# A third pair of r's tiles by seven products, and the mixer's pieces moved together into 44 chunks

## The chip, the cores and the metric

The kernel runs on one core of a Trainium2 chip. The metric is device time in microseconds (us) of one launch, the median of several runs. TensorE (PE) multiplies matrices, VectorE (DVE) and ScalarE (ACT) work elementwise, GpSimd (POOL) does little here, and SyncE (SP) issues nearly all transfers. Each engine takes its instructions strictly in the order in which they were written; semaphores order the engines among each other.

## The reference, cut to what matters

One decoder layer over T = 544 tokens (512 new, 32 sampled), width 2048, fp32. What the change touches is the mixer: a wide input projection whose columns feed gated linear attention (q, k, v, r and a low-rank decay), a short convolution and a chunk MLP.

```python
proj = xn @ w_in
q, k, v, r, a_lr, cb, cc, ch, cu, cv = jnp.split(proj, _split_idx(), axis=-1)
loga = jax.nn.log_sigmoid((a_lr @ w_a2 + b_a).astype(jnp.float32)) / GLA_TAU
o, S_new = gla_chunked((q * (GLA_DK ** -0.5)).reshape(...), k.reshape(...), v.reshape(...), loga.reshape(...), S0)
o = o * lax.rsqrt(jnp.mean(o * o, axis=-1, keepdims=True) + EPS)
o = o * gla_g.reshape(GLA_HEADS, GLA_DV).astype(jnp.float32)
o_gla = o.reshape(B, L, D_GLA).astype(xn.dtype) * jax.nn.silu(r)
...
u = jax.nn.gelu(cu, approximate=False)
vv = layernorm(jax.nn.gelu(cv, approximate=False), cm_ln_g, cm_ln_b)
zc = jnp.einsum('hts,bnshc->bnthc', Wm, vb) + jnp.transpose(cm_bs[:, :T])[None, None, :, :, None]
o_cm = u * zc.reshape(B, L, D_CM)
out = jnp.concatenate([o_gla, o_conv, o_cm], axis=-1) @ w_out
```

Behind it come the residual, a SwiGLU with 5632 hidden columns, and a last norm.

## The kernel before

**Precision.** Every fp32 weight block is split into a rounded high part (ScalarE, a cast into `w_hi`) and a remainder (VectorE, a subtraction into `w_lo`). Each product is then three matmuls: high by high, high by low, low by high.

**The input projection comes in two forms.** A *tile* is 128 output columns. An ordinary tile takes two *chunks* of 8 weight blocks (`tile_half`, `chunk`). One chunk is 8 x 3 x 2 = 48 matmuls over 272 tokens each, so two tiles are four chunks, 192 matmuls. A *seven-product slot* (`kv_product`) does a pair of tiles at once: 12 of the 16 row blocks by Strassen's seven products (7 x 6 x 3 = 126 matmuls), the other four directly in an eighth step (4 x 4 x 3 = 48), together 174. `NR` slots hold tiles of r, six hold k and v; `NQ = NR + 6`. The tiles of r that go through slots are sent to DRAM (`r_dram`) and fetched back later into the last `2 * NR` tiles of `trunk`; ScalarE applies Silu to them there (`R_AT`), and VectorE multiplies them into the attention's output one chunk later, counting `front_done`. The other tiles of r are the last ordinary ones (from `T_R`), with Silu in `gate_tile`.

**The mixer's small work stands between the chunks.** From chunk `C_T` to `C_OUT` TensorE runs the ordinary tiles 17 to `N_IN - 1`. A table of places (`VT_AT`, `Z_AT`, `B_AT`, ...) puts *pieces* of the attention and the chunk MLP behind certain chunks; a place with .5 is the middle of the next chunk. TensorE does a piece's matmuls (`piece`), then VectorE and ScalarE their part (`post`), and `post_v` and `post_a` count what is done. The order that a piece waits for is set in `piece`: `mu` waits for all pieces ahead of it, `("s", 0)` for all up to `var_cm`, `("qs", 0)` for all up to `kdt` and for `s0_split`.

The pieces spoken of below:
- `z0`, `z1`: decay logits. `b0` to `b4`: cumulated decays, transposes and scores. `kdt`: the last transposes of k.
- `qs0` to `qs7`: old state by queries. The state is loaded to `S0` in eighths and split into `s0_hi` (`split_s0_hi`) and `s0_lo` (`split_s0_lo`); these stand at the end of the step two chunks ahead of each `qs`. The first `split_s0_hi` waits for `kdt`, since its room was in use until then.
- `mu`, `var_cm`: mean and variance of the chunk MLP's layer norm.
- `s0`, `s1`: scores and output of the sampled tokens; `s2` to `s9`: the new state. `vvt`, `zc`: chunk MLP. `p0` to `p3`: attention of the pairs. `on0` to `on3`: the heads' norm.

In its step for chunk c, VectorE waits for that chunk's last matmul, takes the finished tile out of PSUM if c is odd (`evac`; one tile in three of the convolution's is followed by `conv_tile`), does the pieces' parts, splits the weights of chunk c + 4 and then a part of the state. So what TensorE waits for can stand behind other work of that queue.

**Transfers.** SyncE issues all of them in program order, waits included, so a transfer that must wait holds up those behind it. Near `C_OUT` the input x is fetched back into `trunk` (`x_back`), in pieces of four tiles.

Of the kernel before, what the change touches and what calls it, by code (L numbers as in the profile page):

```python
# [28 lines left out]
ALU = mybir.AluOpType  # L29
# [4 lines left out]
KT = D // P  # L34
# [16 lines left out]
T_Q, T_CV, T_CONV, T_CU, T_R, N_IN = 1, 17, 21, 33, 37, 41  # L51
# [7 lines left out]
NR = 2  # L59
# [5 lines left out]
C_T = C_Q + NPQ * NQ  # L65
# [20 lines left out]
HEAD_ORDER = (2, 3, 0, 1)  # L86
# [7 lines left out]
B_AT = tuple(C_T + 5 + 2 * i for i in range(5))  # L94
KDT_AT = C_T + 15
QS_AT = tuple(C_T + 17 + i for i in range(8))
MU_AT, VAR_CM_AT, VVT_AT, ZC_AT = C_T + 19.5, C_T + 21.5, C_T + 26, (C_T + 27, C_T + 28)
S_AT = (C_T + 23, C_T + 25) + tuple(C_T + i for i in (29.5, 30.5, 31.5, 32.5, 33.5, 35, 36, 37.5))
P_AT = tuple(C_T + 29 + i for i in range(4))
OSQ_AT = C_T + 32  # L100
ON_AT = tuple(C_T + i for i in (34, 36.5, 38, 40))
# [52 lines left out]
def build(nc, xT, w_alr, w_in, w_kv, w_kc, w_oa, w_out, w_gu, w_d4, w_d3, vecs, wa2, wm, wsbd, bs, s0, cbuf, ident, tri, maskA, maskS,  # L154
          bmask, yT, gla_p, gla_s, conv_o, cmv):
    with ExitStack() as ctx:
# [289 lines left out]
        def slot_out(s):  # L446

            return kv[:, s + 4 if s < NR else s - NR]
# [74 lines left out]
        def _(sp):  # L523
# [96 lines left out]
            for c in range(C_T, C_OUT):  # L620
# [3 lines left out]
                if c == C_T + 13:  # L624
                    sp.wait_ge(inter, number(("z", 1)))
                    load_s0(0)
                    load_s0(1)
                if c == C_T + 14:
                    sp.wait_ge(inter, number(("z", 1)))
                    sp.dma_start(wmm, wm).then_inc(wm_in, 16)  # L630
                    sp.dma_start(bsb, bs.partition_broadcast(P)).then_inc(wm_in, 16)
                for i in range(8):
                    if c == QS_AT[i] + 5:
                        load_s0((i + 2) % 8, (i + 2) // 8)
                    if c == math.ceil(S_AT[2 + i] + 6.5):
                        store_s0(i)
                if c == P_AT[-1] + 10:
                    sp.wait_ge(post_v, parts(V_KINDS, ("p", PAIRS - 1)))
                    sp.dma_start(gla_p.rearrange("h d e -> d h e"), S[:]).then_inc(stored, 16)
                    for i in range(3):  # L640
                        sp.dma_start(trunk[:, 4 * i:4 * i + 4, :], xT[:, 4 * i:4 * i + 4, :]).then_inc(x_back, 16)
# [4 lines left out]
                if c == C_OUT - 1:  # L646
                    sp.wait_ge(front_done, 2 * NR)
                    sp.dma_start(trunk[:, 12:, :], xT[:, 12:, :]).then_inc(x_back, 16)
# [8 lines left out]
                for i in range(6):  # L657
                    if c == math.ceil(S_AT[2 + i] + 6.5):
                        load_s0(i + 2, 1)
# [163 lines left out]
        def _(act):  # L823
# [89 lines left out]
            def gate_tile(i, function):  # L913
                take()
                nc.scalar.activation(tmp[:, i % 2, :], tmp[:, i % 2, :], function).then_inc(silu_r, 1)
# [77 lines left out]
            def op_hi_tile(k):  # L993
                act.wait_ge(mix_done, k - 3)
                act.wait_ge(chunk_done, C_OUT)
                nc.scalar.copy(op_hi[:, k, :], mix[:, MIX_ORDER[k], :]).then_inc(op_h, 1)
# [860 lines left out]
        def _(dve):  # L1857
# [145 lines left out]
            def post(kind, i):  # L2003
# [132 lines left out]
                elif kind == "qs":  # L2136
                    if i % 2 and i < 7:
                        last = query_blocks(i // 2 + 1)
# [140 lines left out]
            def kv_outputs(s, piece):  # L2279
# [3 lines left out]
                if piece == C11:  # L2283
                    if s >= NR + 4:
                        dve.wait_ge(r_out, 16 * (s - NR - 3))
# [135 lines left out]
            for c in range(C_T, C_OUT):  # L2421
# [26 lines left out]
                if c == R_AT + 1:  # L2448
                    dve.wait_ge(post_v, parts(V_KINDS, ("on", 1)))
                    for i in range(2 * NR):  # L2450
                        dve.wait_ge(r_act, i + 1)
                        nc.vector.tensor_tensor(mix[:, 4 + i, :], mix[:, 4 + i, :], trunk[:, KT - 2 * NR + i, :],
                                                ALU.mult).then_inc(front_done, 1)
# [508 lines left out]
```

## Time and profile before

| | |
|---|---|
| median of 3 runs | 2175.64 us (2175.28 to 2175.84) |
| profiled execution, whole | 2175.7 us |
| its span | 2173.9 us |
| TensorE busy | 2163.2 us, 100% of the span |
| VectorE / ScalarE busy | 1707.1 us (79%) / 1014.1 us (47%) |
| seven-product slots | about 64.3 to 238.5 us |
| ordinary tiles with the mixer's pieces | about 238.5 to 590.9 us |
| output projection, first half by seven products | about 590.9 to 675.6 us |

The profiled execution is 1.8 us longer than its span, which is what lies around the first and last instruction. Read the table from the top: an engine at 100% sets the time, and the others matter only where they make it wait. Shares over the whole span hide this, so the stretch of the change has to be read by itself.

### The profile page before, as it was taken

The numbers are of one execution on the slowest core, as the hardware profiler recorded it, in microseconds if no ns is written. First come the engines' busy times: TensorE is split into PE (matmuls) and PEld (weight loads), VectorE is DVE, ScalarE is ACT, GpSimd is POOL, SyncE is SP. The second block draws the span as 40 slices with busy tenths as digits, with TensorE's granted clock in tenths as the row PEclk, the third lists the DMA queues.
The fourth block names the chain that finished last, engine by engine and source line by source line (L and its number), as shares of the span: only waits on it lengthen the run. The fifth ranks groups of instructions, "written<-read, shape, count | busy, mean of one in ns | idle before, by whom it ended". The sixth has DMA issues, their size and how long they took to land.

```text
span 2173.9 us, 40813 instructions
## 1 busy us (share of the span) xinstructions
PE 2163.2 (100%) x17270; PEld 2157.9 (99%) x17270; DVE 1707.1 (79%) x2005; ACT 1014.1 (47%) x1352; POOL 11.6 (1%) x16
## 2 busy tenths in 40 slices
PE   9999999999999999999999999999999999999998
PEld 9999999999999999999999999999999999999998
DVE  7766567656696799878888887888888888887887
ACT  8333352315454555444444544444444445444455
POOL 0000000000000000000000000000000000000001
PEclk9999999999999999999999999999999999999999
DMA  5332233327333434444445445444544885555523
GB/s 192 107 119 86 92 107 117 109 89 256 109 107 108 148 131 153 126 154 156 141 142 159 143 131 159 153 132 142 160 151 157 298 301 213 192 200 190 207 88 131
DMA packets 123167, 328.90 MB, mean 151 GB/s; under 512 B 10878, under 2 KB 51646, under 8 KB 121888
## 3 DMA queue, kind: packets, MB, share of 16 engines
q1 hardware_dynamic: 122224, 326.80, 44.7%
q8 instruction: 85, 1.39, 0.3%
q10 hardware_dynamic: 816, 0.37, 0.1%
q14 instruction: 42, 0.34, 0.0%
HBM read 269.39 MB, written 57.74 MB: 150 GB/s over the span
## 4 chain that ended last, share of the span: by engine, by line
PE 97%; DVE 1%; ACT 1%; issue 1%; DMA 0%; POOL 0%; POOLq 0%; DVEq 0%; ACTq 0%
PE acc L1736 24%; PE acc L1416 20%; PE g L1736 18%; PE acc L1744 12%; PE g L1744 9%; PE acc L1645 3%; PE g L1645 2%; PE acc L1683 2%; PE g L1683 2%; PE g L1637 1%; PE acc L1637 1%; PE g L1443 0%; PE g L1585 0%; PE g L1571 0%; PE g L1578 0%
## 5 line engine op out<-in xcount | busy, mean ns | idle before, releaser
L1221 ACT CAST w_hi<-w_s 128x1024 fp32r<-128x1024 f32 (+1 forms) x204 | 209.1, 1025 | 359.0 <-DVE w_s L2544 350.5
L1736 PE MATMUL g<-op_hi,w_hi 128*128 128x272 f32 x1056 | 272.1, 288 | 0.0
L1736 PE MATMUL acc<-sg_hi,w_hi 128*128 128x272 f32 x1056 | 272.0, 288 | 0.0
L1736 PE MATMUL g<-op_lo,w_hi 128*128 128x272 f32 x1056 | 271.9, 288 | 0.0
L1736 PE MATMUL acc<-op_hi,w_hi 128*128 128x272 f32 x1056 | 271.6, 288 | 0.0
L1736 PE MATMUL acc<-sg_lo,w_hi 128*128 128x272 f32 x1056 | 271.4, 288 | 0.0
L1736 PE MATMUL acc<-op_lo,w_hi 128*128 128x272 f32 x1056 | 271.4, 288 | 0.0
L2519 DVE TENSOR_TENSOR w_lo<-w_s,w_hi 128x1024 fp32r<-128x1024 f32 (+1 forms) x204 | 242.5, 1189 | 12.6 <-ACT w_hi L1221 6.4
L1416 PE MATMUL acc<-op_hi,w_hi 128*128 128x272 f32 x1152 | 241.5, 291 | 0.1
L1416 PE MATMUL acc<-op_hi,w_lo 128*128 128x272 f32 x1152 | 238.3, 288 | 0.0
L1416 PE MATMUL acc<-op_lo,w_hi 128*128 128x272 f32 x1152 | 238.2, 288 | 0.0
L1736 PEld LDWEIGHTS acc<-sg_lo,w_hi 128*128 128x128 f32 x1056 | 198.7, 188 | 0.1
L1736 PEld LDWEIGHTS acc<-op_hi,w_hi 128*128 128x128 f32 x1056 | 198.6, 188 | 0.1
L1736 PEld LDWEIGHTS g<-op_lo,w_hi 128*128 128x128 f32 x1056 | 198.7, 188 | 0.0
L1736 PEld LDWEIGHTS g<-op_hi,w_hi 128*128 128x128 f32 x1056 | 198.5, 188 | 0.1
L1736 PEld LDWEIGHTS acc<-op_lo,w_hi 128*128 128x128 f32 x1056 | 198.6, 188 | 0.0
L1736 PEld LDWEIGHTS acc<-sg_hi,w_hi 128*128 128x128 f32 x1056 | 198.5, 188 | 0.1
L2519 DVE TENSOR_TENSOR w_lo<-w,w_hi 128x1024 fp32r<-128x1024 f32 (+1 forms) x126 | 150.4, 1193 | 49.1 <-ACT w_hi L1221 48.1
L1416 PEld LDWEIGHTS acc<-op_hi,w_hi 128*128 128x128 f32 x1152 | 181.3, 188 | 1.4 <-issue 0.3
L1416 PEld LDWEIGHTS acc<-op_hi,w_lo 128*128 128x128 f32 x1152 | 180.6, 189 | 0.0
L1416 PEld LDWEIGHTS acc<-op_lo,w_hi 128*128 128x128 f32 x1152 | 180.2, 188 | 0.0
L1221 ACT CAST w_hi<-w_raw 128x1024 fp32r<-128x1024 f32 (+1 forms) x115 | 118.4, 1030 | 95.6 <-PE acc L1744 82.7
(395 smaller groups left out, 4882.0 us busy)
## 6 DMA issues: line engine op xcount, KB each, us to landing
w<-w_gu SPq DMA_DIRECT2D x88, 512.0 KB, 3.3
w_raw<-w_gu SPq DMA_DIRECT2D x88, 512.0 KB, 4.1
w_raw<-w_in SPq DMA_DIRECT2D x55, 512.0 KB, 3.5
hf_dram<-hf_hi SPq DMA_DIRECT2D x22, 952.0 KB, 6.4
hf_dram<-hf_lo SPq DMA_DIRECT2D x22, 952.0 KB, 8.7
w_raw<-w_d SPq DMA_DIRECT2D x34, 512.0 KB, 4.0
w<-w_d SPq DMA_DIRECT2D x26, 512.0 KB, 3.3
op_hi<-hf_dram SPq DMA_DIRECT2D x16, 544.0 KB, 7.0
```

The lines of the kernel that those rows point to most:

```text
L1221: nc.scalar.copy(w_hi[:, (C_ST + n) % RING, 0:w], src[:, 0:w]).then_inc(hi_ready, 1)
L1416: last = nc.tensor.matmul(acc[t % 2][:, a, 0:TH], w, x[:, k, a * TH:(a + 1) * TH], start=start and n == 0, stop=stop and n == 2)
L1637: last = nc.tensor.matmul(bank[:, side, 0:TH], w, x, start=False, stop=j == KT - 2 * HQ - 1 and i == 2, skip_group_check=True)
L1645: last = nc.tensor.matmul(banks[idx][:, side, 0:TH], w, x, start=idx < 2 and j == 0 and i == 0, stop=j == HQ - 1 and i == 2, skip_group_ch ...
L1683: last = nc.tensor.matmul(out, w, x, start=idx < 2 and j == 0 and i == 0, stop=j == HP - 1 and i == 2, skip_group_check=True)
L1736: nc.tensor.matmul(out, w_h, x, start=fresh and j == 0 and i == 0, stop=False, skip_group_check=True)
L1744: last = nc.tensor.matmul(out, w_l, x_h, start=False, stop=j == h - 1, skip_group_check=True)
L2519: nc.vector.tensor_tensor(w_lo[:, slot, 0:w], src[:, 0:w], f32(w_hi[:, slot, 0:w]), ALU.subtract)\
```

## The change

`NR` goes from 2 to 3: six of r's eight tiles now go through slots, two stay ordinary. So `N_IN` falls from 41 to 39, there are nine slots in place of eight, and `C_T` to `C_OUT` holds 44 chunks in place of 48. The pieces are moved together into the 44: from `b2` on they stand earlier, and some distances shrink. `kdt` to `qs0` was two chunks and is one. `mu` stood half a chunk behind `qs2` and stands half a chunk behind `qs3`. `var_cm` to `s0` was a chunk and a half and is half a chunk. The places of `z0`, `z1`, `b0` and `b1` (3, 6, 5 and 7) are as before. Tiles that return from DRAM are six, the multiplications by them six; the last head is now head 0 (`HEAD_ORDER`); x comes back as two pieces of four tiles early and two late, where it was three early and one late. Silu's table is loaded ahead of the wait in `gate_tile`.

```diff
-T_Q, T_CV, T_CONV, T_CU, T_R, N_IN = 1, 17, 21, 33, 37, 41
+T_Q, T_CV, T_CONV, T_CU, T_R, N_IN = 1, 17, 21, 33, 37, 39
-NR = 2
+NR = 3
-HEAD_ORDER = (2, 3, 0, 1)
+HEAD_ORDER = (2, 3, 1, 0)
 Z_AT = (C_T + 3, C_T + 6)
-B_AT = tuple(C_T + 5 + 2 * i for i in range(5))
-KDT_AT = C_T + 15
-QS_AT = tuple(C_T + 17 + i for i in range(8))
-MU_AT, VAR_CM_AT, VVT_AT, ZC_AT = C_T + 19.5, C_T + 21.5, C_T + 26, (C_T + 27, C_T + 28)
-S_AT = (C_T + 23, C_T + 25) + tuple(C_T + i for i in (29.5, 30.5, 31.5, 32.5, 33.5, 35, 36, 37.5))
-P_AT = tuple(C_T + 29 + i for i in range(4))
-OSQ_AT = C_T + 32
-ON_AT = tuple(C_T + i for i in (34, 36.5, 38, 40))
+B_AT = tuple(C_T + i for i in (5, 7, 8.5, 10, 11.5))
+KDT_AT = C_T + 13
+QS_AT = tuple(C_T + 14 + i for i in range(8))
+MU_AT, VAR_CM_AT, VVT_AT, ZC_AT = C_T + 17.5, C_T + 19.5, C_T + 23, (C_T + 24, C_T + 25)
+S_AT = (C_T + 20, C_T + 22) + tuple(C_T + i for i in (26.5, 27.5, 28.5, 29.5, 30.5, 32, 33, 34.5))
+P_AT = tuple(C_T + 26 + i for i in range(4))
+OSQ_AT = C_T + 29
+ON_AT = tuple(C_T + i for i in (31, 32.5, 34, 35.5))
 R_AT = C_T + 36
...
-                if c == C_T + 13:
+                if c == C_T + 14:
                     sp.wait_ge(inter, number(("z", 1)))
                     load_s0(0)
...
-                    if c == math.ceil(S_AT[2 + i] + 6.5):
+                    if c == min(math.ceil(S_AT[2 + i] + 6.5), C_OUT - 4):
                         store_s0(i)
...
-                    for i in range(3):
+                    for i in range(2):
                         sp.dma_start(trunk[:, 4 * i:4 * i + 4, :], xT[:, 4 * i:4 * i + 4, :]).then_inc(x_back, 16)
...
                     sp.wait_ge(front_done, 2 * NR)
-                    sp.dma_start(trunk[:, 12:, :], xT[:, 12:, :]).then_inc(x_back, 16)
+                    for i in (2, 3):
+                        sp.dma_start(trunk[:, 4 * i:4 * i + 4, :], xT[:, 4 * i:4 * i + 4, :]).then_inc(x_back, 16)
...
             def gate_tile(i, function):
+                if i == T_R - T_CU:
+                    load_tables(ACT.Silu)
                 take()
...
                 elif kind == "qs":
+                    if i in (4, 6):
+                        dve.wait_ge(post_v, parts(V_KINDS, (("mu", 0) if i == 4 else ("var_cm", 0))))
                     if i % 2 and i < 7:
                         last = query_blocks(i // 2 + 1)
...
                 if c == R_AT + 1:
-                    dve.wait_ge(post_v, parts(V_KINDS, ("on", 1)))
+                    dve.wait_ge(post_v, parts(V_KINDS, ("on", 2)))
```

The order in which instructions stand, at three places, all on VectorE. First, around `kdt` and the first part of the state, before. `L1875` splits weights, `L1944` and `L2183` take a tile out, `L1951` to `L2058` are `kdt`'s part, `L1985` to `L1981` prepare the queries, `L1988` is the low part of the state:

```order
L1875 TENSOR_TENSOR w_lo<-w_raw,w_hi 128x1024 [waits hi_ready,chunk_done]
L1944 TENSOR_TENSOR tmp<-acc,rstd 128x544 [waits mix_done,chunk_done]
L1951 CAST kd<-g 32x512 [waits inter]
L1952 CAST kd<-g 32x512
L1954 TENSOR_TENSOR kd<-g,kd 32x512 [waits v_own]
L1954 TENSOR_TENSOR kd<-g,kd 32x512
L2058 TENSOR_TENSOR egp<-egp 128x4x4 [waits v_own]
L1875 TENSOR_TENSOR w_lo<-w_raw,w_hi 128x1024 [waits hi_ready]
L1985 MEMSET qm 128x1088
L1980 CAST qm<-trunk 128x8x4 [waits v_own]
L1981 TENSOR_TENSOR qm<-trunk,qm 128x8x4 [waits v_own]
L1988 TENSOR_TENSOR s_lo<-S,s_hi 128x1024 [waits s0_split_h]
```

and now (four to six lines further down in the file: `L1992` is the low part of the state, `L1955` to `L2062` `kdt`'s part, `L2243` the convolution's last product):

```order
L1879 TENSOR_TENSOR w_lo<-w_raw,w_hi 128x1024 [waits hi_ready,chunk_done]
L1989 MEMSET qm 128x1088
L1984 CAST qm<-trunk 128x8x4 [waits v_own]
L1985 TENSOR_TENSOR qm<-trunk,qm 128x8x4 [waits v_own]
L1992 TENSOR_TENSOR s_lo<-S,s_hi 128x1024 [waits s0_split_h]
L1948 TENSOR_TENSOR tmp<-acc,rstd 128x544 [waits chunk_done]
L2243 TENSOR_TENSOR mix<-mix,tmp 128x544 [waits acc_free]
L1955 CAST kd<-g 32x512 [waits inter]
L1956 CAST kd<-g 32x512
L1958 TENSOR_TENSOR kd<-g,kd 32x512 [waits v_own]
L1958 TENSOR_TENSOR kd<-g,kd 32x512
L2062 TENSOR_TENSOR egp<-egp 128x4x4 [waits v_own]
```

The low part of the state, and the tile behind it, moved from behind `kdt`'s part to ahead of it.

Second, ahead of `mu` (its first row is the one that waits for `inter` at the end), on VectorE before:

```order
L1944 TENSOR_TENSOR tmp<-acc,rstd 128x544 [waits chunk_done]
L2237 TENSOR_TENSOR mix<-mix,tmp 128x544 [waits acc_free]
L1875 TENSOR_TENSOR w_lo<-w_raw,w_hi 128x1024 [waits inter,hi_ready]
L1988 TENSOR_TENSOR s_lo<-S,s_hi 128x1024 [waits s0_split_h]
L2061 SCALAR_TENSOR_TENSOR mix<-g,mix 128x544 [waits inter]
```

and now, from the convolution's taps on (`L2201` to `L2207`), with `qs3`'s part as `L1984` and `L1985`:

```order
L2201 TENSOR_SCALAR mix<-zp,vec 128x512 [waits v_own]
L2204 SCALAR_TENSOR_TENSOR mix<-zp,vec,mix 128x512 [waits v_own] x2
L2201 TENSOR_SCALAR mix<-zp,vec 128x32 [waits v_own]
L2204 SCALAR_TENSOR_TENSOR mix<-zp,vec,mix 128x32 [waits v_own] x2
L2206 COPY cst<-zp 128x2 [waits v_own]
L2207 COPY cst<-zp 128x16
L1984 CAST qm<-trunk 128x8x4 [waits inter]
L1985 TENSOR_TENSOR qm<-trunk,qm 128x8x4 [waits v_own]
L1879 TENSOR_TENSOR w_lo<-w_raw,w_hi 128x1024 [waits hi_ready]
L1992 TENSOR_TENSOR s_lo<-S,s_hi 128x1024 [waits s0_split_h]
L2065 SCALAR_TENSOR_TENSOR mix<-g,mix 128x544 [waits inter]
```

A whole convolution tile and a part of a `qs` piece now stand right ahead of `mu`.

Third, behind `var_cm`, on VectorE before (`L2079` and `L2084` are its part):

```order
L2079 SCALAR_TENSOR_TENSOR mix<-mix,vec,lnb 128x544 [waits post_a,inter]
L2079 SCALAR_TENSOR_TENSOR mix<-mix,vec,lnb 128x544 x3
L2084 TENSOR_SCALAR mix<-mix,vec 128x544 [waits v_own]
L2084 TENSOR_SCALAR mix<-mix,vec 128x544 x3
L1980 CAST qm<-trunk 128x8x4 [waits inter,chunk_done]
L1981 TENSOR_TENSOR qm<-trunk,qm 128x8x4 [waits v_own]
L1875 TENSOR_TENSOR w_lo<-w_raw,w_hi 128x1024 [waits hi_ready]
L1988 TENSOR_TENSOR s_lo<-S,s_hi 128x1024 [waits s0_split_h]
L1944 TENSOR_TENSOR tmp<-acc,rstd 128x544 [waits chunk_done]
```

and now, where `s0`'s part (`L2150` to `L2153`) follows at once:

```order
L2083 SCALAR_TENSOR_TENSOR mix<-mix,vec,lnb 128x544 [waits post_a,inter]
L2083 SCALAR_TENSOR_TENSOR mix<-mix,vec,lnb 128x544 x3
L2088 TENSOR_SCALAR mix<-mix,vec 128x544 [waits v_own]
L2088 TENSOR_SCALAR mix<-mix,vec 128x544 x3
L2150 COPY ovm<-idn 32x128 [waits post_v,chunk_done,inter]
L2150 COPY ovm<-idn 32x128
L2152 MEMSET ovm 32x128
L2153 COPY_PREDICATED ovm<-mS,g 32x128 [waits v_own]
```

Five instructions and a chunk that stood between `var_cm` and `s0` are gone from there.

## Rows read from the trace of the kernel before

**Rows 1.** The page's busy time of each engine.

```profile
PE 2163.2 (100%) x17270; PEld 2157.9 (99%) x17270; DVE 1707.1 (79%) x2005; ACT 1014.1 (47%) x1352; POOL 11.6 (1%) x16
```

**Rows 2.** Waits of TensorE: engine, line, releaser: us in total, times, longest.

```profile
PE g L1436 <- POOL onesf L797: 1.2, 1, 1.2
PE g L1829 <- DVEq L2850: 0.3, 1, 0.3
```

**Rows 3.** Chain of waits in time: start, us, what. Slots, then a chunk.

```profile
81.61 4.48 PE g L1645 x36
...
103.39 4.48 PE g L1645 x36
...
238.55 6.02 PE acc L1416 x48
```

**Rows 4.** Chain of waits: kdt, qs0, half a chunk, var_cm, three products.

```profile
351.94 0.44 PE g L1475 x4
...
364.41 0.97 PE g L1585 x8
...
394.24 3.03 PE acc L1416 x24
397.26 0.92 PE g L1468 x4
...
597.27 9.04 PE acc L1683 x72
```

**Rows 5.** VectorE in order of time: start, us, line, operation [idle before].

```profile
337.20 0.72 DVE L1944 TENSOR_TENSOR tmp<-acc,rstd 128x544 f32<-128x544 f32 x1 [0.41 <-PE acc L1416]
337.96 0.72 DVE L2237 TENSOR_TENSOR mix<-mix,tmp 128x544 f32<-128x544 f32 x1
...
352.62 0.67 DVE L1951 CAST kd<-g 32x512 fp32r<-32x512 f32 x1
...
355.43 0.17 DVE L2058 TENSOR_TENSOR egp<-egp 128x16 f32<-128x16 f32 x1
...
360.81 1.22 DVE L1988 TENSOR_TENSOR s_lo<-S,s_hi 128x1024 fp32r<-128x1024 f32 x1
```

**Rows 6.** ScalarE in order of time: high part of the state.

```profile
353.01 1.04 ACT L911 CAST s_hi<-S 128x1024 fp32r<-128x1024 f32 x1
```

**Rows 7.** VectorE in order of time: queries; then a convolution tile.

```profile
388.71 0.17 DVE L1980 CAST qm<-trunk 128x32 fp32r<-128x32 f32 x1
388.92 0.19 DVE L1981 TENSOR_TENSOR qm<-trunk,qm 128x32 fp32r<-128x32 f32 x1
...
408.21 0.72 DVE L1944 TENSOR_TENSOR tmp<-acc,rstd 128x544 f32<-128x544 f32 x1 [1.33 <-PE acc L1416]
...
413.12 0.44 DVE L2144 COPY ovm<-idn 32x128 f32<-32x128 f32 x2
```

**Rows 8.** VectorE in order of time: var_cm's part.

```profile
399.65 2.88 DVE L2079 SCALAR_TENSOR_TENSOR mix<-mix,vec,lnb 128x544 f32<-128x544 f32 x4 [2.81 <-ACT lnb L962]
402.56 1.74 DVE L2084 TENSOR_SCALAR mix<-mix,vec 128x544 f32<-128x544 f32 x4
```

**Rows 9.** VectorE in order of time: forms of the output projection.

```profile
565.03 1.29 DVE L2330 TENSOR_TENSOR fa_lo<-mix,fa_hi 128x1088 fp32r<-128x1088 f32 x1 [1.61 <-ACT fa_hi L1007]
...
598.77 1.29 DVE L2344 TENSOR_TENSOR op_lo<-mix,op_hi 128x1088 fp32r<-128x1088 f32 x1
```

**Rows 10.** Transfers from 480 to 600 us: KB each, median us to landing.

```profile
w_raw<-w_in SPq DMA_DIRECT2D x11, 512.0 KB, 3.8
trunk<-xT SPq DMA_DIRECT2D x4, 1088.0 KB, 9.8
```

**Rows 11.** Windows: length, busy PE, PEld, DVE, ACT, POOL, PEclk, DMA share, GB/s.

```profile
554.90:560.90 6.00, 6.00 (x50) 6.00 (x50) 2.68 (x3) 2.88 (x3) 0.00 (x0) 1.00 0.89 347
...
2165.00:2169.00 4.00, 0.00 (x0) 0.00 (x0) 3.22 (x6) 1.07 (x3) 2.82 (x3) 1.00 0.70 263
...
2170.00:2172.00 2.00, 0.00 (x0) 0.00 (x0) 0.00 (x0) 0.00 (x0) 0.10 (x1) 0.50 1.04 404
```

More of the change, by code:

```diff
@@ L446, in slot_out @@
         def slot_out(s):
-            return kv[:, s + 4 if s < NR else s - NR]
+            return kv[:, s + 6 - NR if s < NR else s - NR]
         def slot_kv(n):
@@ L627, in _ @@
                     load_s0(1)
-                if c == C_T + 14:
+                if c == C_T + 15:
                     sp.wait_ge(inter, number(("z", 1)))
@@ L657, in _ @@
                 for i in range(6):
-                    if c == math.ceil(S_AT[2 + i] + 6.5):
+                    if c == min(math.ceil(S_AT[2 + i] + 6.5), C_OUT - 4):
                         load_s0(i + 2, 1)
@@ L993, in op_hi_tile @@
             def op_hi_tile(k):
-                act.wait_ge(mix_done, k - 3)
+                if k < KT - 2:
+                    act.wait_ge(mix_done, k - 3)
                 act.wait_ge(chunk_done, C_OUT)
@@ L2283, in kv_outputs @@
                 if piece == C11:
-                    if s >= NR + 4:
-                        dve.wait_ge(r_out, 16 * (s - NR - 3))
+                    if s >= 6:
+                        dve.wait_ge(r_out, 16 * (s - 5))
                     nc.vector.tensor_tensor(y[:, 0, 0:TH], pa[:, q, 0:TH], rstd[:, 0:TH], ALU.mult).then_inc(kv_read, 1)
@@ L2448, in _ @@
                 if c == R_AT + 1:
-                    dve.wait_ge(post_v, parts(V_KINDS, ("on", 1)))
+                    dve.wait_ge(post_v, parts(V_KINDS, ("on", 2)))
                     for i in range(2 * NR):
                         dve.wait_ge(r_act, i + 1)
-                        nc.vector.tensor_tensor(mix[:, 4 + i, :], mix[:, 4 + i, :], trunk[:, KT - 2 * NR + i, :],
-                                                ALU.mult).then_inc(front_done, 1)
+                        m = mix[:, KT // 2 - 2 * NR + i, :]
+                        nc.vector.tensor_tensor(m, m, trunk[:, KT - 2 * NR + i, :], ALU.mult).then_inc(front_done, 1)
                 if c == MIX_SINGLE_AT:
```

## The prediction

> **What bounds the kernel now.** I read the busy times first. TensorE is busy 2163.2 of 2173.9 us [rows 1]. Then the waits of TensorE: there are two in the whole span, 1.2 us at the very start and 0.3 us near the end [rows 2]. So in all the stretches that the change touches TensorE never waits, and the time is the sum of its matmuls. What shortens its work shortens the kernel; what the other engines do counts only where a wait that was covered comes into the open. The chain of waits says the same: slot follows slot and chunk follows chunk with no gap [rows 3]. The profiled execution took 2175.7 us, 1.8 more than its span and 0.06 more than the median of 2175.64; I work from the former and take the 0.06 off at the end.
>
> **What is removed.** Slots repeat from 81.61 to 103.39 in the chain, 21.78 us each; the eight of them have one form. An ordinary chunk of 48 matmuls takes 6.02 us [rows 3]. Four chunks go, 24.08 us, and a slot comes, 21.78 us. That is -2.30 us on the engine that sets the end. By count it is 192 - 174 = 18 matmuls of 6.02 / 48 = 0.125 us, -2.26 us. I take -2.3. This is the most that the change can give, and it is 0.11% of the time, below the 0.2% (4.35 us) that a measurement of this kernel can tell from no change.
>
> The new slot costs VectorE and ScalarE more than four chunks' splits did, but they have idle time in that stretch and the slots before it had no gap, so I put it at nothing; from the eight slots as they ran it could be at worst a few tenths. The third pair to DRAM and the six Silus and products in place of four lie beside TensorE.
>
> **What is moved: every TensorE wait again.** The pieces stand closer, so for each I compared the moment when TensorE gets there with the moment when the queue ahead of the part it waits for is done, with the durations of before. Most keep a cover: the waits of the p and s pieces stand exactly as far apart as they did, and `b2`, `b3`, `b4`, `vvt` and `zc` arrive later than what they wait for. Three do not.
>
> *First, `qs0`, a chunk behind `kdt`.* It waits for `kdt`'s part on VectorE. The first cast of the state's high part on ScalarE waits for `kdt`'s matmuls; before, VectorE had `kdt`'s part ahead of the state's low part, now the low part is ahead, and with it the tile of that step. Counting from the end of `kdt`'s matmuls: the cast 1.04 [rows 6], with about 0.1 to start; the low part 1.22; the tile and its product 0.72 + 0.72; `kdt`'s part from 352.62 to 355.60, 2.98 [rows 5]. The sum is 6.8 us. TensorE is there after one chunk, 6.02 [rows 3]. Wait: 0.7 to 0.8, I take 0.7, since neighbours in the rows overlap by some 0.1. VectorE itself gets to the low part at about the time when the cast is done, because a convolution tile and `b4`'s part stand ahead in the same queue; where it is later, the wait grows by as much. Bounds 0.3 to 1.7.
>
> *Second, `mu`, half a chunk behind `qs3`.* It waits for all parts ahead, so for `qs3`'s. VectorE does that behind the tile of the step for `C_T + 17`, which is one with a convolution. Such a tile runs from 408.21 to 413.12, 4.91 us, and the queries take 388.71 to 389.11, 0.40 [rows 7]: 5.35 us from the chunk's end. TensorE is there after `qs3` and half a chunk, 0.97 + 3.03 = 4.0 [rows 4]. Wait: 1.4 with the release. Before, `mu` stood behind `qs2`, in a step without a convolution, and the wait was covered. Bounds 1.1 to 1.7.
>
> *Third, `s0`, behind `var_cm`, half a chunk and `qs6`.* It waits for `var_cm`'s part. `var_cm`'s matmuls ended at 398.18 [rows 4] and its last VectorE instruction at 404.30 [rows 8]: 6.12 us of square root by logarithm, then eight operations, all in a row. TensorE now gets there after 3.03 + 0.97 = 4.0. Wait: 2.15, with the release 2.2. Before, a whole chunk more stood between. Bounds 1.8 to 2.6.
>
> Behind `s0` VectorE has its own small part and a split, and the split is for a chunk four further on, so nobody else is held up. A wait also gives the other two engines time, so the three do not add to later ones.
>
> **Near `C_OUT`.** Six products with the returned tiles in place of four put VectorE some 1.3 us later at the handover, and with the tighter table I find the forms of the output projection (565.03, 26.0 us ahead of `C_OUT`) about 1.7 us later against it [rows 9]. The narrowest cover is the form for the fifth product. It was ready at 600.06 [rows 9]. TensorE started that product at 606.31 - 3.01 = 603.30, since the three products in the row end at 606.31 and take 9.04 [rows 4]: 3.2 us of cover. That leaves 1.5, so nothing. Loading Silu's table ahead gives time to a ScalarE that nobody waits for there: nothing. The same holds for the x tiles that now return late, with the proviso of the second rival.
>
> **Sum.** -2.3 + 0.7 + 1.4 + 2.2 = +2.0 us, 2177.7 on the profiled execution, 2177.6 as a median. The work that was saved is given back, and somewhat more, in three new waits. The title's word of second decay logits ahead of the second decay piece moves nothing: both places are as before.
>
> **A rule of the Trainium skill.** TensorE's clock was granted at 1.00, the 2.4 GHz level, in every stretch with matmuls that I looked at, and stayed at 1.00 over 4 us without a matmul, from 2165 to 2169 us at the kernel's end; it was 0.50, the 1.2 GHz level, from 2170 on [rows 11]. By that my longest wait, 2.2 us, leaves the clock where it is. The Trainium skill, in "TensorE: Matmul & The Clock Gate", section "Part 1: The HAM clock gate", says that the default is throttled and that activity releases it. It speaks against any change that opens gaps on TensorE; by the row, gaps of this length are not enough, and the trace does not show a gap between matmuls that would decide it.
>
> **Rivals.**
>
> *The waits are not there: 2173.4.* If VectorE's queue is ahead of my count, or the three waits stay under a few tenths each, the saving stands: 2175.64 - 2.3 = 2173.3 to 2175. For it: no wait of TensorE in this stretch in the trace [rows 2]. Against it: `mu` and `s0` are short by more than a microsecond, and their terms are a few instructions in a row with measured lengths.
>
> *The late x tiles hold up the last weights: slower, 2182.0.* SyncE now issues two transfers of 1088 KB behind `front_done`, about 27 us ahead of `C_OUT`, and the weights of the last chunk after them. If each took its 9.8 us after the other, and the weights 3.8 [rows 10], they would land 27.3 - 19.6 - 3.8 = 3.9 us ahead of `C_OUT`. They are needed 6.0 us ahead for the chunk, and 2.3 sooner for the splits (1.05 and 1.22), so 8.3. It would cost 4.4 us on top: 2182.0, which is slower by 0.29%. It decides from the point where the two take over 15 us together. Against it: 347 GB/s moved in the window in which the single one was under way [rows 11], and at that rate two take 6.4 us. The Trainium skill, in "DMA: Bandwidth & Descriptors", section "Issuing engines are not separate DMA queues", says that all transfers run on the same 16 DMA engines and interleave; by it the weights share with the x tiles even where they are not behind them. With the rate of the row both orders end in time.
>
> *The clock falls in a wait.* If a wait of 2 us brought the 1.2 GHz level, a chunk would take up to twice 6.02, so up to +6.0: 2183.6. The window behind the last matmul speaks against it.
>
> *The change doesn't do what it says.* The number of slots, chunks and pieces in the order of the instructions is as described, so I leave it no chance of its own.
>
> **How the numbers follow.** Forecast (three waits, 3.3 to 5.5 us together; 2176.3 to 2179.3): 0.60. No or small waits, 2173.3 to 2176.3: 0.22. Late x tiles, 2179.5 to 2182: 0.08. Clock: 0.02. Waits that I did not find, +1 to +5 on top: 0.08. The predicted time is 2177.6. The range runs from 2173.3, the whole saving, to 2181.0; it leaves out the upper part of the last three cases. Slower by over 0.2% (above 2180.0) takes most of the last three cases: 0.13. Faster by over 0.2% (below 2171.3) would need twice what the count of matmuls gives: 0.01. The rest, 0.86, is within 0.2%.
>
> **What would show it.** TensorE's matmuls fall by 18 in the whole, and nine slots of 21.8 us stand in the chain. Between `C_T` and `C_OUT`, TensorE's waits list three lines: the first matmul of `qs0` released by the last copy of `kdt`'s part, that of `mu` by the queries' subtraction, that of `s0` by `var_cm`'s last addition, with about 0.7, 1.4 and 2.2 us. The granted clock stays at 1.00 there. Wrong would be: no such lines; one of over 3 us; a wait for a transfer, or for weights, in the last chunks or at the first products of the output projection.

## The result and the profile after

The changed kernel takes 2180.08 us (median of 15 executions, 2178.06 to 2182.59), the kernel before 2175.64 (15 executions, 2175.24 to 2176.29). The ratio is 1.002, 95% interval 1.0013 to 1.0027: slower by 4.4 us, which is 0.2%. The forecast was 2177.6 with a range to 2181.0. The direction of the mechanism was right and its size too small. The profiled execution took 2180.65 us with a span of 2177.8; the three waits are in it as forecast, and three further terms are not in the forecast: longer pieces behind two of the waits, a low clock behind the third, and a longer output projection.

Busy times, against [rows 1]; 18 matmuls fewer, yet TensorE is busy as long as before:

```profile
PE 2163.1 (99%) x17252; PEld 2157.4 (99%) x17252; DVE 1714.7 (79%) x2016; ACT 1017.1 (47%) x1360; POOL 11.9 (1%) x16
```

TensorE's waits, against [rows 2]:

```profile
PE g L1596 <- DVE mix L2088: 2.2, 1, 2.2
PE g L1472 <- DVE qm L1985: 1.4, 1, 1.4
PE g L1440 <- POOL onesf L798: 1.2, 1, 1.2
PE g L1589 <- DVE egp L2062: 0.7, 1, 0.7
PE acc L1687 <- ACT acc L1032: 0.3, 1, 0.3
```

`s0` waits for `var_cm`'s last addition, `mu` for the queries, `qs0` for `kdt`'s last product: the three waits, their releasers and their lengths are those of the forecast. The fifth line is new: a seed that ScalarE copies for the output projection.

The chain at the second and third wait (start, us, what), against [rows 4]. It shows what the list of waits cannot: the pieces that follow a wait.

```profile
395.15 0.20 DVE qm L1985
...
395.40 1.18 PE g L1472 x4
396.58 3.02 PE acc L1420 x24
...
410.54 0.93 PE g L1472 x4
...
412.92 2.88 DVE mix L2083 x4
...
415.83 1.75 DVE mix L2088 x4
...
417.62 0.44 PE g L1596 x8
418.06 7.72 PE acc L1420 x48
425.79 0.96 PE g L1589 x8
```

The chunk behind `s0` takes 7.72 us where an ordinary one takes 6.02 [rows 3]. Behind `s0` the chunk is somewhat longer in the kernel before too, where no wait stands ahead of it:

```profile
409.13 0.37 PE g L1592 x8
409.50 6.24 PE acc L1416 x48
```

So about 1.5 us of the 7.72 are new. The windows over the chunk (length, busy PE, PEclk, DMA share, GB/s) say why:

```profile
417.00:418.00 1.00, 0.38 (x9) 1.00 0.00 0
418.00:419.00 1.00, 1.00 (x10) 1.00 0.00 0
419.00:420.00 1.00, 1.00 (x8) 0.61 0.07 16
420.00:421.00 1.00, 1.00 (x6) 0.50 0.00 0
421.00:422.00 1.00, 1.00 (x7) 0.50 0.59 115
422.00:423.00 1.00, 1.00 (x7) 0.69 0.97 385
```

The granted clock is still 1.00 when the wait ends, at 417.62, and for 1.6 us of matmuls behind it; then it is 0.50, the 1.2 GHz level. The four windows are short of 1.00 by 0.39, 0.50, 0.50 and 0.31 us of full clock, 1.7 together, which at half the clock is a stretch of 3.4 us (419.2 to 422.6). The chunk is longer by 1.5, nearly all of that.

**Where the time went, by stages.** Four instructions of TensorE mark the stages in every kernel: the first product of the first slot, the first product of the output projection that goes to `acc`, the first chunk product behind that projection's slots, and the first of the last group. In order of time (start, us, line, operation), before:

```profile
64.12 0.29 PE L1645 MATMUL acc<-op_hi,w_hi 128*128 128x272 f32 x1
...
591.10 0.29 PE L1683 MATMUL acc<-fa_hi,w_hi 128*128 128x272 f32 x1
...
675.41 0.42 PE L1416 MATMUL acc<-op_hi,w_hi 128*128 128x272 f32 x2
...
2163.35 1.54 PE L1829 MATMUL acc<-hst,onesf 128*128 128x272 f32 x6
```

and after:

```profile
64.08 0.29 PE L1649 MATMUL acc<-op_hi,w_hi 128*128 128x272 f32 x1
...
595.10 0.29 PE L1687 MATMUL acc<-fa_hi,w_hi 128*128 128x272 f32 x1
...
679.95 0.42 PE L1420 MATMUL acc<-op_hi,w_hi 128*128 128x272 f32 x2
...
2167.29 1.54 PE L1833 MATMUL acc<-hst,onesf 128*128 128x272 f32 x6
```

Stage A (slots, chunks and pieces) is the second start less the first: 526.98 before, 531.02 after, +4.04. Stage B (the output projection's slots) is 84.31 before, 84.85 after, +0.54. Stage C is 1487.94 and 1487.34; in the other kernels below it lies between 1487.33 and 1487.75. Half of the 0.6 is the wait of 0.3 us near the end [rows 2], which no other profile has; no experiment aims at the rest. Of the 5.0 us between the two profiled executions, 1.0 lies outside the span (2.9 us in place of 1.8). The table gives A and B of every profiled execution and the times of all; its last column is the kernel before, measured again beside that row.

| kernel | median us (lowest to highest) | A less 526.98 | B less 84.31 | before beside it |
|---|---|---|---|---|
| before | 2175.64 (2175.24 to 2176.29) | 0 | 0 | 2175.64 |
| after | 2180.08 (2178.06 to 2182.59) | +4.04 | +0.54 | 2175.64 |
| after, once more | 2180.53 (2178.39 to 2182.84) | +2.51 | +1.23 | 2175.45 |
| `s0` a chunk later | 2177.72 (2175.80 to 2178.23) | +0.24 | +0.66 | 2175.64 |
| `mu` waits for less | 2178.83 (2177.31 to 2179.51) | +2.37 | +1.22 | 2175.64 |
| `kdt`'s part first | 2180.04 (2178.17 to 2181.98) | +2.13 | +2.43 | 2175.64 |
| third wait alone | 2178.07 (2177.08 to 2180.73) | +0.49 | +1.73 | 2175.45 |
| all three mended | 2174.65 (2174.02 to 2176.62) | -1.80 | +0.54 | 2175.64 |
| the same, no table ahead | 2175.68 (2175.52 to 2177.22) | -1.80 | +2.00 | 2175.37 |
| the same, `r` sooner | 2177.05 (2175.75 to 2178.2) | -1.80 | +2.65 | 2175.45 |
| before, `s0` sooner | 2178.27 (2177.48 to 2180.58) | +2.21 | +0.01 | 2175.37 |
| `s0` ahead of `qs6` | 2182.2 (2179.21 to 2183.88) | +3.50 | +0.66 | 2175.37 |
| `s0` directly behind `var_cm` | 2185.62 (2185.03 to 2186.82) | +8.06 | +2.35 | 2175.37 |

The rows below "after" have eleven executions each, the last two six and five. One execution of 7470.4 us of the kernel with `s0` a chunk later, and one of 3006.76 us of the kernel before beside it, lie outside everything else and are left out of the ranges. One profile is one execution; its A and B show where that execution's time lies, and the median shows what is usual. Rows with different values in the last column are best compared by what each has over the kernel before beside it. The first slot starts between 64.08 and 64.57 in all of them, and what lies outside the span is 1.7 to 2.9 us.

### The profile page after: what moved, and what is told of

Read it like the earlier page. It is cut to its first block, busy times and chain, and to the rows that moved or that the text cites. A ratio compares the mean times of both kernels' runs of the same rounds, so it can differ in the third digit from the quotient of the medians.

```text
span 2177.8 us, 40793 instructions
## 1 busy us (share of the span) xinstructions
PE 2163.1 (99%) x17252; PEld 2157.4 (99%) x17252; DVE 1714.7 (79%) x2016; ACT 1017.1 (47%) x1360; POOL 11.9 (1%) x16
## 4 chain that ended last, share of the span: by engine, by line
PE 96%; DVE 2%; issue 1%; ACT 1%; DMA 0%; POOL 0%; POOLq 0%; DVEq 0%; ACTq 0%; SPq 0%
PE acc L1740 24%; PE g L1740 18%; PE acc L1420 17%; PE acc L1748 12%; PE g L1748 9%; PE acc L1649 4%; PE g L1649 3%; PE acc L1687 2%; PE g L1641 1%; PE acc L1641 1%; PE g L1687 1%; DVE w_lo L2312 0%; PE g L1447 0%; PE g L1575 0%; PE g L1582 0%
## 5 line engine op out<-in xcount | busy, mean ns | idle before, releaser
L1740 PE MATMUL acc<-op_hi,w_hi 128*128 128x272 f32 x1056 | 271.7, 289 | 0.0
L1740 PE MATMUL acc<-op_lo,w_hi 128*128 128x272 f32 x1056 | 271.5, 288 | 0.0
L1420 PE MATMUL acc<-op_hi,w_hi 128*128 128x272 f32 x1088 | 228.8, 292 | 0.0
L1420 PE MATMUL acc<-op_hi,w_lo 128*128 128x272 f32 x1088 | 225.9, 289 | 0.0
L1420 PE MATMUL acc<-op_lo,w_hi 128*128 128x272 f32 x1088 | 225.7, 289 | 0.0
L1740 PEld LDWEIGHTS acc<-op_lo,w_hi 128*128 128x128 f32 x1056 | 199.1, 189 | 0.0
L1740 PEld LDWEIGHTS acc<-op_hi,w_hi 128*128 128x128 f32 x1056 | 198.8, 188 | 0.1
L1420 PEld LDWEIGHTS acc<-op_hi,w_hi 128*128 128x128 f32 x1088 | 172.1, 189 | 1.1
L1420 PEld LDWEIGHTS acc<-op_hi,w_lo 128*128 128x128 f32 x1088 | 171.5, 190 | 0.0
L1420 PEld LDWEIGHTS acc<-op_lo,w_hi 128*128 128x128 f32 x1088 | 170.9, 189 | 0.0
```

The costliest lines, as they stand in the source:

```text
L1420: last = nc.tensor.matmul(acc[t % 2][:, a, 0:TH], w, x[:, k, a * TH:(a + 1) * TH], start=start and n == 0, stop=stop and n == 2)
L1740: nc.tensor.matmul(out, w_h, x, start=fresh and j == 0 and i == 0, stop=False, skip_group_check=True)
```

## Experiments

**The third wait.** `s0` one chunk later:

```diff
-S_AT = (C_T + 20, C_T + 22) + ...
+S_AT = (C_T + 21, C_T + 22) + ...
```

> Changed kernel with the matmuls of s0 one chunk later (at C_T + 21, behind qs7). My theory: the 2.2 us wait for var_cm's part goes, and with it the stretch at clock 0.50 that cost 1.7 us in the next chunk, so 3.9 us less than the changed kernel: 2176.2 as a median, the times within 0.5 us of each other, the granted clock 1.00 from 415 to 426 us, and the waits of qs0 (0.7) and mu (1.4) as they were. Rival A, the fall of the clock comes from the thin work of the whole stretch (three waits and short pieces), not from this wait: the clock still falls to 0.50 and only 2.2 us go, 2177.9. Rival B, the wait only moves to s1, now one chunk behind s0: no more than 1 us goes, 2179.

Measured: 2177.72, ratio to before 1.0009 (1.0000 to 1.0018). TensorE's waits between `C_T` and `C_OUT`:

```profile
PE g L1472 <- DVE qm L1985: 1.4, 1, 1.4
...
PE g L1589 <- DVE egp L2062: 0.7, 1, 0.7
```

The wait is gone and did not move to `s1`, so rival B falls. Every window from 414 to 428 us shows a clock of 1.00, which goes against rival A. Stage A is 3.80 less than after's, which is the 2.2 of the wait and the 1.5 of the low clock. As a median only 2.4 go, not the 3.9 that I expected. Not every execution of the changed kernel has the fall, as a later run shows. Nor are the times within 0.5 us of each other: four lie from 2175.80 to 2176.84, the profiled one among them, and six from 2177.62 to 2178.23, with a mean clock of 0.999. That speaks for something other than this wait and the clock, which makes some executions longer by about 1.5 us; the profile is of the shorter kind and can't name it.

**The second wait.** In the function that issues a piece:

```diff
+                elif kind == "mu":
+                    before = order[:number(("qs", 2))]
```

> Changed kernel with mu waiting for the parts up to qs2's in place of all parts ahead. My theory: the 1.4 us wait goes and nothing else changes: VectorE takes up mu's part at the same moment, so var_cm, s0 and the 2.2 us wait stand as they did or the wait grows a little, because TensorE comes sooner to it, by up to 1.4 us; the clock falls to 0.50 behind it as before. If var_cm's chain is bound by TensorE (its matmuls start it), 1.4 us go: 2178.7. Rival A, the waits stand in for one another (s0's end is set by VectorE): the wait at s0 grows by 1.4 and nothing goes, 2180.1. Rival B, the 1.4 us wait is part of what brings the clock down: the clock stays at 1.00 and 3.1 us go, 2177.0.

Measured: 2178.83, 1.2 us under the changed kernel. The wait is gone, and the third is as long as it was. The second line is `mu`'s piece in the chain:

```profile
PE g L1598 <- DVE mix L2090: 2.2, 1, 2.2
```

```profile
394.50 0.92 PE g L1472 x4
```

`mu`'s four products take 0.92 us here and 1.18 behind the wait. Stage A, with a fall in both profiles, is 1.67 less than after's: 1.4 for the wait and 0.26 for the piece.

Nor do the waits stand in for one another: `var_cm`'s part is started by TensorE's matmuls, so it starts sooner and ends sooner. Windows behind the wait (same columns):

```profile
416.00:417.00 1.00, 0.52 (x9) 0.87 0.00 0
417.00:418.00 1.00, 1.00 (x5) 0.50 0.08 16
...
420.00:421.00 1.00, 1.00 (x9) 0.92 0.70 160
```

The clock falls without `mu`'s wait ahead. So the 1.4 us wait is not needed for a fall, and rival B is out; the chunk takes 7.66 us. The wait ends at 416.48, and the window from 416 has 0.87: here the fall comes 0.3 us behind the wait's end, in the changed kernel's profile 1.6 us behind it.

**The first wait.** VectorE does `kdt`'s part before the low part of the first state; the zeroing of the queries stays where it was:

```diff
                     query_blocks(0)
+                    return
+                state_lo(i)
+
+            def state_lo(i):
                 dve.wait_ge(s0_split_h, i + 1)
...
+                if c == KDT_AT:
+                    state_lo(0)
                 split_lo(c + 4, c + 4)
```

> Changed kernel with VectorE doing kdt's part ahead of the low part of the first decode state, as in the kernel before. My theory: the queue from the end of kdt's matmuls to the end of what qs0 needs is tile 1.4, kdt's part 3.0, low part 1.2 = 5.6 us, under the chunk of 6.0: the 0.7 us wait goes and the others stay, 2179.4. Rival, the queue is longer by what stands in front of it on VectorE (a convolution tile and b4's part): a wait of 0.3 to 0.7 stays, 2179.8 to 2180.1.

Measured: 2180.04, no difference from the changed kernel's 2180.08, and where the rival put it. TensorE still waits 0.4 us at `qs0`, now for the low part. So the edit could bring some 0.3 us, and the profiled execution lost that elsewhere. In it the clock stayed at 1.00 behind the 2.2 us wait, and yet the time was 2180.96: stage B is 2.43 longer than before's. VectorE's waits from 500 to 582 us point at a decode state that landed late:

```profile
DVE S L2171 <- DMA S<-s: 2.3, 1, 2.3
```

and VectorE in order of time shows what became of it:

```profile
571.12 1.29 DVE L2340 TENSOR_TENSOR fa_lo<-mix,fa_hi 128x1088 fp32r<-128x1088 f32 x1 [1.99 <-ACT fa_hi L1011]
```

The forms start 22.46 us ahead of the first output product (593.58), where they start 24.24 ahead in the changed kernel and 26.07 in the one before. TensorE then waits 1.9 us for seeds. Two later profiles show the same: a state late by 1.7 us (third wait alone; forms 23.05 ahead, B +1.73) and by 2.2 us (`s0` directly behind `var_cm`; 22.58 ahead, B +2.35). In the two profiles of the changed kernel VectorE does not wait for a state at this place.

**All three.**

> All three edits at once: s0 one chunk later, mu waiting for qs2's part, kdt's part first on VectorE. My theory: no wait of TensorE is left between C_T and C_OUT, the clock stays at 1.00 there, and of the 4.3 us of waits and 1.7 us of clock nothing is left: 2175.64 - 2.3 for the slot in place of four chunks + 0.3 for the seed at the handover = 2173.6, faster than the kernel before by 0.09%. Rival A, the nine-slot form has a cost that no wait shows (more outside the span, a slower slot): 2175 to 2176. Rival B, the waits only move to the next pieces (s1, var_cm): 2176 to 2178.

Measured: 2174.65 (2174.02 to 2176.62), ratio 0.9998 (0.9989 to 1.0007); it is 1 us under before as a median, and that is not told from no change. TensorE's waits are all of these:

```profile
PE g L1440 <- POOL onesf L798: 1.2, 1, 1.2
PE acc L1420 <- ACT w_hi L865: 1.1, 1, 1.1
PE g L1591 <- DVE s_lo L1998: 0.4, 1, 0.4
PE acc L1689 <- ACT acc L1032: 0.3, 1, 0.3
```

The second is at the start of the kernel. Stage A is 1.80 less than before's, that is -2.3 for the slot in place of four chunks, 0.4 for the wait at `qs0` that is left and 0.2 for `qs0`'s first piece, which takes 1.18 us behind that wait and 0.97 before [rows 4]: -1.7, to 0.1 us. So the saving on TensorE is real and of the forecast size, and the waits were what ate it. Rival B falls: no wait moved. My time of 2173.6 was too low by 1.0 and rival A's, 2175 to 2176, too high by 0.35, and its reason doesn't hold: no slot is slower. Stage B is 0.54 longer, as in the changed kernel's first profile, more than the 0.3 that I had counted. The two stages make -1.3, and the medians differ by -1.0.

**The wait alone, in the kernel before.**

```diff
-S_AT = (C_T + 23, C_T + 25) + ...
+S_AT = (C_T + 22, C_T + 25) + ...
```

> Kernel before (eight slots, 48 chunks) with only s0 moved one chunk earlier, to C_T + 22, so that it stands half a chunk and one qs piece behind var_cm as in the changed kernel. My theory: this spacing alone makes the wait of 2.2 us, without any of the other parts of the change, and the wait alone can bring TensorE's clock down: +2.2 when the clock stays at 1.00 (2177.8), up to +3.9 when it falls to 0.50 behind the wait (2179.5); median 2178 to 2179.5, with more spread than the kernel before. Rival: the wait in the changed kernel also needs its nine slots or its tight table: no wait here, 2175.6. Second rival, the clock falls only with the shorter waits ahead of it: +2.2 in every run, spread as of before.

Measured: 2178.27 (2177.48 to 2180.58), ratio 1.0014 (1.0005 to 1.0023). The wait is there:

```profile
PE g L1592 <- DVE mix L2084: 2.2, 1, 2.2
```

Stage A is longer by 2.21 and nothing else is in it; the clock stayed at 1.00 in the profiled execution. The spacing alone makes the wait. The median is 2.9 us over the kernel before beside it, 0.7 more than the wait. The executions lie within 3.1 us, the kernel before's within 1.7 (2174.99 to 2176.65). That would fit a fall in some executions, but the one profile of this kernel has none, and the kernel with `s0` a chunk later has a spread of 2.4 us without such a wait. So it is not shown here.

**The wait longer, twice.** `s0` ahead of `qs6` in its step (the order of the kinds in the plan), and `s0` at `C_T + 19.5`, in `var_cm`'s half chunk:

> Changed kernel with s0 ahead of qs6 in its step: the same point of release, so a wait of 3.1 to 3.2 us in place of 2.2, and qs6 (0.97) behind it. Cost of the wait: +0.97. My theory: the clock falls behind it more often than behind 2.2 us, +0.97 and up to +1.7 more: 2181 to 2183, and 0.50 in the profile behind the wait. Rival: the clock's fall doesn't hang on the wait's length: 2181.05.

> Changed kernel with s0 directly behind var_cm, in the same half chunk: TensorE stands for all of var_cm's part, 6.1 us, in one piece. My theory: 6.2 - 2.2 = +4.0 for the wait, and the clock now falls in every execution, with a loss of 1.7 to 3.4 us as against 1.7 in some of those of the changed kernel: 2184 to 2187. The chunk's second half and qs6 that stood ahead of the wait come behind it at the low clock. Rival: the fall of the clock hangs on chance or on the earlier waits and not on the length: 2184.1 and a spread as of the changed kernel.

The kind `s` now stands ahead of `qs` where the plan is made; for the other, the edit is

```diff
-S_AT = (C_T + 20, C_T + 22) + ...
+S_AT = (C_T + 19.5, C_T + 22) + ...
```

Measured, the first: 2182.2 from six executions, 6.8 us over the kernel before beside it, where the changed kernel has 4.4. So 2.4 us come on top, and the longer wait is 0.97 of that. The wait is as computed:

```profile
PE g L1596 <- DVE mix L2088: 3.2, 1, 3.2
```

But the clock stayed at 1.00 in every window of its profile, and that execution took 2179.21, the lowest of all. So a wait of 3.2 us need not bring the fall; whether the other five, 2181.15 to 2183.88, had one is not shown. The second: 2185.62, the wait is 6.2 us, and the clock falls inside it:

```profile
414.00:415.00 1.00, 0.00 (x0) 0.91 0.55 221
415.00:416.00 1.00, 0.00 (x0) 0.50 0.00 0
...
420.00:421.00 1.00, 1.00 (x7) 0.50 0.00 0
421.00:422.00 1.00, 1.00 (x7) 0.68 0.00 0
```

It lasts twice as long (414.8 to 421.6, 6.8 us in place of 3.4), but nearly half of that is the wait itself, which ends at 417.96, so it costs TensorE 1.6: stage A is 5.55 over that of the changed kernel without a fall (+2.51), 3.96 of it from the longer wait. Its five times lie within 1.8 us, the fifteen of the changed kernel within 4.5. That fits a fall in every execution, but only one is profiled.

**Third wait alone, and the changed kernel again.** The first has the edits of the second and third experiment together.

> Changed kernel with the waits of qs0 and mu mended and the third, of s0 for var_cm's part, left. My theory: the third wait alone can bring the clock down, so the time is that of the kernel with all three mended plus 2.2 for the wait plus about 1 us, the mean of executions in which the clock falls (1.7 and more) and of those in which it stays: 2177.8, and between 2176.9 and 2179.5 for single executions. Rival, the clock needs the shorter waits ahead of it: 2176.9 with a spread of under 1.5 us.

> The changed kernel once more, nothing edited, for a second profile and more times beside the others of this call. My theory: the same three waits to 0.1 us; the clock behind the third one falls or stays, from execution to execution. Median 2180.1; times within 0.5 us of each other would speak against a fall that comes and goes.

Measured: 2178.07 (2177.08 to 2180.73) and 2180.53 (2178.39 to 2182.84). The changed kernel's second profile has the same three waits (2.2, 1.4, 0.7) and no fall. Windows at the same place as above, and the chunk from its chain:

```profile
419.00:420.00 1.00, 1.00 (x11) 1.00 0.07 16
420.00:421.00 1.00, 1.00 (x11) 1.00 0.00 0
421.00:422.00 1.00, 1.00 (x11) 1.00 0.52 90
```

```profile
417.62 0.44 PE g L1596 x8
418.06 6.20 PE acc L1420 x48
```

To a hundredth the chunk starts at the same time as in the first profile, and takes 6.20 in place of 7.72: a fall costs 1.52 us, and stage A differs by 1.53. The same program with the same waits has it or has it not. With the third wait alone the median is 0.3 us from the forecast, but two of eleven executions lie above the 2179.5 that I set as the upper end. The profile has no fall. The spread is 3.7 us, over the rival's limit of 1.5, but part of it is stage B's (+1.73 in the profile), so this does not settle whether the shorter waits ahead make a fall more frequent. Of six profiles with a wait of 2.2 us two have the fall.

**The handover: one edit undone, one tried.** The three mended waits, without the load of Silu's table ahead:

```diff
-                if i == T_R - T_CU:
-                    load_tables(ACT.Silu)
```

> The kernel with all three waits mended, but without the load of Silu's table ahead of its wait. My prediction put this edit at nothing. Since TensorE waited 0.3 us for a seed at the handover to the output projection, nothing of the cover that I counted is left there: the load of 1.28 us now comes between the tile and the casts on ScalarE, and VectorE waits for those casts. My theory now: the seeds come about 1.3 us later and TensorE waits 1 to 2 us more: 2175.7 to 2176.5 against 2174.65. Rival, the prediction's word: nothing, 2174.65.

Measured: 2175.68, which is 1.0 us over the same kernel with it, and 1.3 when each is taken against the kernel before beside it. Stage A is the same to a hundredth, stage B 1.46 longer. ScalarE in order of time:

```profile
584.03 1.28 ACT L916 ACT_TABLE_LOAD   x1 [6.81 <-DVEq L2254]
585.33 0.66 ACT L916 ACTIVATE tmp<-tmp 128x544 f32<-128x544 f32 x1
```

The load of 1.28 us now stands between the release and the tile, and TensorE waits 1.5 us for seeds in place of 0.3. The prediction's "nothing" is refuted; what I expected of this run holds. And `r`'s Silu and products a chunk sooner:

```diff
-R_AT = C_T + 36
+R_AT = C_T + 35
```

> The kernel with all three waits mended, and r's Silu and products one chunk sooner (R_AT = C_T + 35 in place of 36). My theory: the handover to the output projection has no cover left because the forms wait for r's six products (ScalarE's cast waited 1.7 us for them); one chunk sooner they are done when the forms' step comes, VectorE is about 1.7 us earlier at the handover, and TensorE's waits for seeds there (0.3 us in the profile, more where a state tile lands late) go: 2174.3 to 2174.0 as a median, with less spread above it. Rival, the handover's time is set by the wait for w_oa's block, which stays: nothing, 2174.65. Second rival, r's tiles or Silu's table now come at a worse place and hold up ScalarE's splits: 2175 or more.

Measured: 2177.05, 2.4 us slower than without (2.6 against the kernel before beside each). My theory fell, the second rival holds: ScalarE now has Silu's six tiles and a table load ahead of the last norm's two functions, the tiles behind shift, and the forms start later, not sooner:

```profile
566.59 1.29 DVE L2342 TENSOR_TENSOR fa_lo<-mix,fa_hi 128x1088 fp32r<-128x1088 f32 x1 [1.51 <-ACT fa_hi L1011]
```

That is 22.81 us ahead of the first output product (589.40). Over all profiles with the table loaded ahead or with the forms as before: forms 26.1 ahead, B +0.0 (two profiles); 24.2 ahead, +0.54 to +1.23 (six); 22.5 to 23.1 ahead, +1.73 to +2.65 (four). So later forms go with a longer stage B, by about a microsecond for each from 24.2 on, but profiles with the same lead differ by up to 0.7 us, and what makes that difference is open.

## Why the prediction was right and where it fell short

*What bounds the kernel, and the saving.* Right. The work saved on TensorE is 2.3 us: the page's busy time of TensorE in the second profile of the changed kernel is 2160.9 against 2163.2, and the kernel with mended waits keeps it in stage A, but for what is left at `qs0`.

*The three waits.* Right, each to 0.1 us, with the releasers named. Each also went by the edit that aims at it, though of `qs0`'s half stayed. One small thing is missing in the way they were added: two of the pieces behind a wait are themselves longer. `mu`'s four products take 1.18 us behind theirs and 0.92 without it, the first `qs` piece 1.22 and 0.97 before [rows 4]:

```profile
368.81 1.22 PE g L1589 x8
```

Together that is the 0.5 by which stage A without a fall (+2.51) exceeds the forecast's +2.0. Behind the third wait nothing is added at full clock: `s0` and its chunk take 0.44 + 6.20 us with it and 0.37 + 6.24 in the kernel before.

*The clock.* The range held, but the step that failed is "By that my longest wait, 2.2 us, leaves the clock where it is", and with it the chance of 0.02. The row that it leant on, 1.00 from 2165 to 2169 us without a matmul [rows 11], showed one gap in one execution; a gap that size was not enough there, and I took it for never enough. The runs show a fall behind a wait of 2.2 us in two of six profiles, none behind 3.2 in the one profile of it, and one behind 6.2. It costs 1.5 us, not the up to 6.0 that I gave the rival, since the low clock lasts only 3.4 us. In the 26 times of the changed kernel two groups stand apart: ten from 2178.06 to 2179.03, sixteen from 2179.85 to 2182.84, the former with a mean granted clock of 0.999, the latter with 0.998. The forecast of 2177.6 with the 0.5 above lies near the first; the median is in the second. That the second group is the executions with a fall fits the two profiles (0.999 without, 0.998 with), but it is not shown. The mean clock is a coarse sign: the profiled executions with the 3.2 us wait, with `kdt`'s part first and with the third wait alone have 0.998 and no window under 1.00 ahead of the kernel's end. And a time in the second group needs no fall: with `kdt`'s part first, 2180.96 came from stage B. The Trainium skill, in "TensorE: Matmul & The Clock Gate", section "Part 1: The HAM clock gate", says that activity is what releases the clock, and also that the monitor behind it does not start with the kernel, so that the same kernel differs from run to run. The two profiles of the changed kernel fit that: one chunk, started at 418.06 in both, with and without the low level.

*Near `C_OUT`.* The term "That leaves 1.5, so nothing" failed too. The forms came 1.8 us later against the end of the chunks (26.07 to 24.24), as said, but I had taken the form for the fifth product as the narrowest cover. It was the seed that ScalarE copies for the second slot (the wait lies between 620 and 624 us in the profile), and with later forms that for the first slot too (between 600 and 604 in the profile with `kdt`'s part first). The seed for the second slot has no cover left: stage B is 0.54 and 1.23 longer in the two profiles. It follows that Silu's table ahead is worth 1.0 to 1.5 us there, not nothing, and that lateness from further up arrives at TensorE.

*"The three do not add to later ones"* held for stage A. In stage B it is not lateness of TensorE that counts but of VectorE against it: when TensorE's waits are taken away VectorE comes no sooner than before against it, and a state's transfer that lands 2.3 us late is paid there.

*What the sum should have been.* Stage A with a fall is -2.3 + 4.3 for the waits + 0.5 for the pieces behind them + 1.5 for the clock = +4.0, as measured; stage B adds 0.5 to 1.2. That the measured 2180.08 lies within the range is owed to room that I gave to late x tiles and to waits not found: it is above the 2179.3 that ends the forecast case, and in the part above 2180.0, to which I gave 0.13.

*The rivals.* No waits: out, all three are there. Late x tiles: the transfer of one chunk's weights, issued 0.9 us behind the two of 1088 KB, took 8.0 us, where the median was 3.8 [rows 10]:

```profile
w_raw<-w_in SPq DMA_DIRECT2D x1, 512.0 KB, 8.0
```

That fits a sharing of the engines, as the Trainium skill says in "DMA: Bandwidth & Descriptors", section "Issuing engines are not separate DMA queues". TensorE waits for this chunk's weights in no profile. Waits that I did not find: there is one, 0.3 to 0.6 in the changed kernel, under the bound of 1 that I gave the case, though stage B as a whole is 1.23 longer in one profile. Two other kernels (`mu` waits for less; `r` sooner) also wait 0.3 us for the low part of a weight block between 640 and 660 us.

## What to carry to other kernels

When a kernel's bounding engine has no waits, shortening its work by 2 us is worth nothing until the spacing of every piece that depends on another engine has been counted again; here one trace was enough to count three waits to 0.1 us. Count the same way at the next stage, through every engine's seeds and copies and not only the operands. And price a wait on TensorE above its own length: the piece behind it can be longer (by 0.25 us here, at two waits of three), and the clock may fall behind it in some executions (1.5 us here), which one profile can miss.

## What the runs showed of the hardware

A wait of TensorE of 2.2 us can be followed by some 3.4 us at 0.50, the 1.2 GHz level, and the same program can run through the same wait at 1.00: 7.72 and 6.20 us for the same chunk started at 418.06 in both. The fall came 1.6 us behind the wait's end in one profile, 0.3 us behind it in another, and inside a wait of 6.2 us, 3 us after it began. Waits of 0.7 and 1.4 us, in all profiles that had them, left 1.00. What decides in one execution is open: the same waits ahead gave both, a wait of 3.2 us had no fall in its one profile, and a fall came without the 1.4 us wait ahead.
